# A two-layer retention and DeltaNet trunk on one core: two TensorE turns of the DeltaNet steps go by VectorE and DRAM, two sums of squares go to ScalarE

## The chip, the cores and the metric

The kernel runs on one core of a Trainium2 chip. The core has five engines that run side by side, each with its own queue of instructions: TensorE (PE in the profile, with its weight loads as PEld), VectorE (DVE), ScalarE (ACT), GpSimd (POOL) and SyncE (SP), which only issues transfers here. ScalarE's queue issues transfers too. Engines wait for each other by semaphores. The metric is the device time of one execution in microseconds; lower is better.

## What is computed

Two layers work on 1024 tokens of width 1024. Each normalises its input, multiplies it by one wide projection, and feeds a retention branch (4 heads) and a gated DeltaNet branch (8 heads of 128 channels). Both are gated, lifted, merged and projected back. The change touches the DeltaNet branch, cut here to what matters:

```python
qkv = silu(causal_conv(concat([dq, dk, dv]), conv_w))
q = l2norm(q) * DN_DK ** -0.5;  k = l2norm(k)
# chunks of tokens, per head: L from k k^T, beta and decay; (I + L) solved by blocks for u and w
v_new = u_n - w_n @ state
o     = q_dec @ state + attn @ v_new
state = state * exp(g_last) + k_dec^T @ v_new
o_d = o * rsqrt(mean(o * o) + EPS) * dn_gain      # normed per token and head
o_d = o_d * silu(dz)                              # the gate
```

## The kernel before

All the large products are three-pass ones: each operand is split in a high and a low part, and three matmuls of 128x512 stand for one (lines 866, 868 and 870). Channels lie on partitions and tokens along the row, except inside the DeltaNet steps, where a chunk of 128 tokens lies on partitions.

The DeltaNet branch runs as **units**, half a head each (512 tokens, four chunks). A layer has one unit `first`, then for 7 heads an `even` and an `odd` unit, then `even_last` and `odd_last`. Unit t does two things at once: it runs the recurrence of half head t, and it prepares half head t + 1 (Gram matrix of the keys, the blockwise solve, the query-key product). The order of all of it is written out by hand in `unit_schedule`: 24 slots for a unit, each with some steps of the two strands and two pieces ("fill") of the projection matmuls of later heads. Every engine walks the same list and does its own part of each step; between steps it waits only for the semaphores named in its part. So a step's place in the list is its place in the queue of every engine that takes part in it. TensorE writes the projections to two PSUM banks in turn, and ScalarE or VectorE ("evac", "z_silu") must empty a bank before it is written again.

The steps that the change touches:

- `ks`, `xu`, `so` (slots 0 to 11): the recurrence over four chunks. TensorE (lines 1171, 1182, 1195 to 1202) alternates with VectorE (`ks` at 2299, `so` at 2309 and 2314) and ScalarE (`xu`, 1620).
- `kt` (slot 2): TensorE turns four 128x128 blocks of the next keys into token rows (line 1109, by the helper at 849); VectorE multiplies them, out of PSUM, with the decay into `kd` (2205). The recurrence of the next unit needs `kd`, and so does `level_v` 0.
- `vs` (slot 2): a 128x4 product on VectorE (2208). `solve` (slots 3 to 7): 30 small VectorE instructions (2280, 2283), behind the load of the blocks of L from DRAM by SP.
- `qt` (slot 4): TensorE turns the queries, ScalarE squares them (1615), VectorE sums (`qe`, 2213).
- `osq`, `og`, `on` (slots 12 to 14): ScalarE squares the unit's output out of PSUM (1625), VectorE sums along the row (2319) and adds, GpSimd takes the power (2676), VectorE multiplies into `on` (2329).
- `ob` (slot 15): TensorE turns `on` back to channels on partitions (1205), VectorE multiplies it with the gate `sz` (2333). `store` (slot 18): ScalarE's queue sends it to `o_scratch` in DRAM.
- `gram`, `diag`, `keys`, `nl` (slots 15 to 17): the Gram matrix of the keys after next on TensorE (1104) and its scalings on VectorE (2163 to 2191). `on` and the product of `diag` share one buffer.

GpSimd splits weights (2579, three times a unit), scales the queries (2672, at `qt`) and masks (2659, 2661). SP loads weights (655), rows and the blocks of L.

## Time and profile before

| | |
|---|---|
| median of three runs | 2646.9 us (2643.08 to 2647.69) |
| the profiled execution: span from first to last instruction | 2644.2 us |
| median above that span | 2.7 us |
| TensorE busy | 2620.6 us, 99% |
| VectorE busy | 1761.1 us, 67% |
| ScalarE, GpSimd busy | 704.5 and 798.6 us, 27% and 30% |
| TensorE's granted clock, mean | 0.999 of full speed |

The profile lists one execution. Its span has no further time of its own around it in the page, so it stands beside the median of the runs. A busy time is the sum of an engine's instructions; matmuls overlap in the array, so their durations can't be added up. L849 is line 849 of the kernel. `arena` is the one large SBUF buffer from which most tiles are cut, `work` and `dense_ps` are PSUM.

### The profile page before, as it was taken

Reading aid. Unit: us, or ns where it says so; the run is one execution under the profiler, and the core shown is the slowest. Engines: PE = TensorE matmul, PEld = TensorE weight load, DVE = VectorE, ACT = ScalarE, POOL = GpSimd, SP = SyncE. Lnnn points to the kernel's source line nnn. Section 1 sums busy time; section 2 is a strip of 40 time slices with the busy share of each in tenths; the row PEclk is TensorE's granted clock in tenths of the full one; section 3 lists DMA queues with packets and bytes.
Section 4 is the critical chain, followed back from the end, with each engine's and each line's share of the span. In section 5 each row is a group of like instructions: output and inputs, shape, how many; then the busy total and the mean of one; then the engine's idle time right before and its main releaser. Section 6 shows DMA issues by size and latency. Waiting matters only on the chain.

```text
span 2644.2 us, 40210 instructions
## 1 busy us (share of the span) xinstructions
PE 2620.6 (99%) x14874; PEld 2238.1 (85%) x14874; DVE 1761.1 (67%) x3972; ACT 704.5 (27%) x1440; POOL 798.6 (30%) x451
## 2 busy tenths in 40 slices
PE   8999999999999999999999999999999999999998
PEld 6888888888888899888877888888888998898887
DVE  7878777877755555434577778777877555653333
ACT  5333333333311212200143333333332221231001
POOL 3123333333312212334512233332322122132453
PEclk9999999999999999999999999999999999999999
DMA  5321222122211112433533222222222111133344
GB/s 174 100 85 58 81 69 85 53 86 65 85 50 43 41 35 76 130 96 120 157 90 88 77 74 69 73 77 72 67 77 73 43 51 43 41 106 100 99 135 152
DMA packets 293416, 217.79 MB, mean 82 GB/s; under 512 B 31747, under 2 KB 246101, under 8 KB 292965
## 3 DMA queue, kind: packets, MB, share of 16 engines
q1 hardware_dynamic: 259620, 159.07, 20.9%
q10 hardware_dynamic: 33600, 56.15, 6.3%
q8 instruction: 119, 1.95, 0.3%
q14 instruction: 77, 0.62, 0.1%
HBM read 176.30 MB, written 38.86 MB: 81 GB/s over the span
## 4 chain that ended last, share of the span: by engine, by line
PE 92%; DVE 3%; DMA 2%; issue 1%; ACT 1%; SPq 0%; POOL 0%; ACTq 0%; DVEq 0%; POOLq 0%
PE dense_ps L866 23%; PE dense_ps L870 23%; PE dense_ps L868 23%; PE work L849 3%; PE dense_ps L890 2%; PE dense_ps L891 2%; PE dense_ps L892 2%; PE work L1145 1%; PE work L1182 1%; PE work L1202 1%; PE work L1121 1%; PE work L1104 1%; PE work L1171 1%; PE work L1195 1%; PE work L1156 1%
## 5 line engine op out<-in xcount | busy, mean ns | idle before, releaser
L866 PE MATMUL dense_ps<-act_hi,w_hi 128*128 128x512 f32 x2552 | 1048.3, 411 | 1.7 <-DVE w_lo L1797 0.8
L870 PE MATMUL dense_ps<-act_hi,w_lo 128*128 128x512 f32 x2552 | 998.4, 391 | 0.0
L868 PE MATMUL dense_ps<-act_lo,w_hi 128*128 128x512 f32 x2552 | 997.3, 391 | 0.0
L2579 POOL TENSOR_TENSOR w_lo<-w_raw,w_hi 128x1024 fp32r<-128x1024 f32 x162 | 400.1, 2470 | 1024.5 <-ACT w_hi L1429 582.7
L870 PEld LDWEIGHTS dense_ps<-act_hi,w_lo 128*128 128x128 f32 x2552 | 479.0, 188 | 105.8
L866 PEld LDWEIGHTS dense_ps<-act_hi,w_hi 128*128 128x128 f32 x2552 | 481.0, 188 | 86.9 <-POOL act_lo L2600 2.3
L868 PEld LDWEIGHTS dense_ps<-act_lo,w_hi 128*128 128x128 f32 x2552 | 481.5, 189 | 78.8 <-issue 0.5
L1973 DVE SCALAR_TENSOR_TENSOR arena<-arena,cols 128x512 f32<-128x512 f32 x288 | 244.3, 848 | 6.1
L1429 ACT ACTIVATE w_hi<-w_raw 128x1024 fp32r<-128x1024 f32 x94 | 99.1, 1054 | 330.5 <-PE dense_ps L870 310.5
L1419 ACT ACTIVATE arena<-dense_ps 128x512 f32<-128x512 f32 x96 | 57.2, 596 | 258.5 <-PE dense_ps L870 258.5
L849 PE MATMUL work<-mk,arena 128*128 128x128 f32 x768 | 112.1, 275 | 7.9 <-DMA arena<-in_x 7.9
L2280 DVE TENSOR_TENSOR arena<-arena 128x60 f32<-128x60 f32 (+14 forms) x480 | 99.9, 208 | 20.2 <-DMA arena<-l_scratch 7.8
L892 PE MATMUL dense_ps<-v_later_lo,act_hi 128*128 128x256 f32 x384 | 107.9, 281 | 0.0
L890 PE MATMUL dense_ps<-v_later_hi,act_hi 128*128 128x256 f32 x384 | 107.9, 281 | 0.0
L891 PE MATMUL dense_ps<-v_later_hi,act_lo 128*128 128x256 f32 x384 | 107.9, 281 | 0.0
L849 PEld LDWEIGHTS work<-mk,arena 128*128 128x128 f32 x768 | 91.8, 142 | 17.7 <-issue 5.2
L2283 DVE TENSOR_TENSOR arena<-arena 128x60 f32<-128x60 f32 (+14 forms) x480 | 92.4, 192 | 16.5
L2666 POOL TENSOR_TENSOR arena<-arena,negh 128x4 f32<-128x4 f32 x32 | 33.0, 1032 | 230.1 <-DVE arena L2180 230.1
L866 PE MATMUL dense_ps<-o_hi,w_hi 128*128 128x512 f32 x256 | 99.6, 389 | 0.0
L868 PE MATMUL dense_ps<-o_lo,w_hi 128*128 128x512 f32 x256 | 99.6, 389 | 0.0
L870 PE MATMUL dense_ps<-o_hi,w_lo 128*128 128x512 f32 x256 | 99.6, 389 | 0.0
L1620 ACT ACTIVATE arena<-work 128x128 f32<-128x128 f32 x128 | 34.9, 273 | 229.7 <-PE work L1182 224.4
(262 smaller groups left out, 4094.7 us busy)
## 6 DMA issues: line engine op xcount, KB each, us to landing
w_raw<-in_w_in SPq DMA_DIRECT2D x138, 512.0 KB, 3.8
arena<-l_scratch SPq DMA_DIRECT2D x64, 256.0 KB
arena<-gate_scratch ACTq DMA_DIRECT2D x64, 256.0 KB, 2.7
gate_scratch<-arena ACTq DMA_DIRECT2D x36, 256.0 KB, 2.0
w_raw<-in_w_out SPq DMA_DIRECT2D x18, 512.0 KB, 3.7
o_scratch<-arena ACTq DMA_DIRECT2D x32, 256.0 KB, 2.2
w_raw<-in_w_up_dn SPq DMA_DIRECT2D x16, 512.0 KB, 3.6
arena<-o_scratch ACTq DMA_DIRECT2D x32, 256.0 KB, 3.7
```

The costliest lines, as they stand in the source:

```text
L849: mm = eng.transpose(wk[bank][:, c * P:(c + 1) * P], src, ident)
L866: eng.matmul(dense_ps[:, to, :], w_hi[:, slot, k, :], hi[:, k, seg], start=(k == 0), stop=False)
L868: eng.matmul(dense_ps[:, to, :], w_hi[:, slot, k, :], lo[:, k, seg], start=False, stop=False)
L870: mm = eng.matmul(dense_ps[:, to, :], w_lo[:, slot, k, :], hi[:, k, seg], start=False, stop=(k == KT - 1))
L890: eng.matmul(dst, act_hi[:, k, tok], hi[:, k, :], start=(k == 0), stop=False)
L891: eng.matmul(dst, act_lo[:, k, tok], hi[:, k, :], start=False, stop=False)
L892: mm = eng.matmul(dst, act_hi[:, k, tok], lo[:, k, :], start=False, stop=(k == KT - 1))
L1429: eng.activation(w_hi[:, slot, :, :], w_raw[:, :, :], ACT.Copy).then_inc(w_hi_ok.sem, 1)
L1973: eng.scalar_tensor_tensor(out=acc[:, i % 2, :], in0=src, scalar=wcol, in1=acc[:, i % 2, :], op0=ALU.mult, op1=ALU.add).then_inc(conv_s.se ...
L2280: eng.tensor_tensor(xm[:, :, 0:left], column, xs[:, :, k:k + 1].to_broadcast([P, CPH, left]), ALU.mult).then_inc(sv_s.sem, 1)
L2283: eng.tensor_tensor(xs[:, :, k + 1:BASE], xs[:, :, k + 1:BASE], xm[:, :, 0:left], ALU.add)\
L2579: eng.tensor_tensor(w_lo[:, slot, :, :], w_from[second][:, :, :], w_hi[:, slot, :, :].bitcast(F32), ALU.subtract)\
```

## The change

In the units `even` and `odd`, the turn of the normed output (`ob`) leaves TensorE; the turn of the keys (`kt`) leaves it in all `odd` units and in the `even` ones from the second head on. In their place VectorE transposes the 32x32 blocks of both (`turn_o` in slot 15, `turn_k` in slot 17), ScalarE's queue stores the blocks to DRAM in four transfers that put each block at its turned place (`put`, slot 18; runs of 32 floats, 128 B) and, when these have landed, loads both tiles back as whole rows (`get`, slot 21; runs of 512 B). The next unit's `kd` product reads the keys from there, and the gate product of the output (`late_ob`) is done in slot 3 of the next unit, its store (`late_store`) in slot 10. The two squares are done by ScalarE in four pieces of 128x128 with a sum each, and VectorE's two row sums go. Three semaphores are merged into one to make room; this adds no wait.

```diff
@@ unit_schedule (kinds that end in "last" keep "ob" and "store")
-        at(18, "store")
+            at(18, "store")
+        if kind in ("even", "odd"):
+            at(3, "late_ob")
+            at(10, "late_store")
+        elif kind == "even_last":
+            at(1, "late_ob")
+            at(3, "late_store")
...
-        begin(15, 1, ("ob",))
+        begin(15, 1, ("turn_o",))
+        at(17, "turn_k")
+        at(18, "put")
+        at(21, "get")
@@ TensorE
                         elif what == "kt":
+                            if kind == "odd" or kind == "even" and h:
+                                continue
...
                             if t is not None:
-                                eng.wait_ge(ob_ok.sem, ob_ok.after(t, 0))
+                                eng.wait_ge(on_ok.sem, on_ok.after(t, 0))
@@ ScalarE
-                            eng.activation(sq, wk[1 + nb][:, :], ACT.Square).then_inc(sq_ok.sem, 1)
+                            for c in range(CPH):
+                                ins = eng.activation(sq[:, c * P:(c + 1) * P], wk[1 + nb][:, c * P:(c + 1) * P], ACT.Square,
+                                                     accum_out=qss[:, c:c + 1])
+                            ins.then_inc(sq_ok.sem, 1)
...
+                        elif what == "put":
+                            u = back(l, h, b)
+                            ms = slice(0, 2 * CPH * CPH)
+                            eng.wait_ge(on_ok.sem, on_ok.after(t, BACK + 1))
+                            eng.wait_ge(back_in.sem, back_in.after(u, 0))
+                            for i in range(CPH):
+                                rows = slice(32 * i, 32 * i + 32)
+                                eng.dma_start(back_dram[ms, :, rows].rearrange("m r s -> r m s"), turned[rows, ms, :])\
+                                   .then_inc(back_st.sem, 16)
+                        elif what == "get":
+                            u = back(l, h, b)
+                            eng.wait_ge(back_st.sem, back_st.after(u, 64))
+                            eng.wait_ge(kd_ok.sem, kd_ok.after(tn, 1))
+                            eng.wait_ge(ob_ok.sem, ob_ok.after(t, 0))
+                            eng.dma_start(tokens[:, 0:2].rearrange("p x c t -> p (x c) t"),
+                                          back_dram[0:2 * CPH * CPH, :, :].rearrange("(m j) r d -> (j r) m d", j=CPH))\
+                               .then_inc(back_in.sem, 16)
@@ VectorE ("diag" of the next keys, then "kt", "qe", "og" and the new steps)
+                            if step[1] and t is not None:
+                                eng.wait_ge(on_ok.sem, on_ok.after(t, 2))
...
-                            eng.tensor_tensor(kd[nb], chunks(4), per_token(hs[:, 3, ns_of]), ALU.mult).then_inc(kd_ok.sem, 1)
+                            if kind == "odd" or kind == "even" and h:
+                                eng.wait_ge(back_in.sem, back_in.after(back(l, h, b) - 1, 16))
+                                src = tokens[:, BACK_K]
...
+                            eng.tensor_tensor(kd[nb], src, per_token(hs[:, 3, ns_of]), ALU.mult).then_inc(kd_ok.sem, 1)
...
-                            eng.tensor_reduce(qss, sq.rearrange("p (c t) -> p c t", c=CPH), mybir.AxisListType.X, ALU.add)\
-                               .then_inc(qe_s.sem, 1)
...
-                            eng.tensor_reduce(og[:, 0, :], osq.rearrange("p (c t) -> p c t", c=CPH), mybir.AxisListType.X,
-                                              ALU.add).then_inc(og_s.sem, 1)
...
+                        elif what == "turn_o":
+                            eng.wait_ge(on_ok.sem, on_ok.after(t, 1))
+                            eng.transpose(turned_of(BACK_O), on.rearrange("p c t -> p (c t)")).then_inc(on_ok.sem, 1)
+                        elif what == "turn_k":
...
+                            eng.transpose(turned_of(BACK_K), kqv[:, 0, b * HALF:(b + 1) * HALF]).then_inc(on_ok.sem, 1)
+                        elif what == "late_ob":
...
+                            eng.wait_ge(back_in.sem, back_in.after(back(l, h, b) - 1, 16))
+                            eng.scalar_tensor_tensor(out=sz[:, seg], in0=tokens[:, BACK_O].rearrange("p c t -> p (c t)"),
+                                                     scalar=dngh[:, 0:1], in1=sz[:, seg],
+                                                     op0=ALU.mult, op1=ALU.mult).then_inc(ob_ok.sem, 1)
```

## Rows read from the trace of the kernel before

**Rows 1.** The page: busy us (share of span) xinstructions; chain of waits by engine.
```profile
PE 2620.6 (99%) x14874; PEld 2238.1 (85%) x14874; DVE 1761.1 (67%) x3972; ACT 704.5 (27%) x1440; POOL 798.6 (30%) x451
...
PE 92%; DVE 3%; DMA 2%; issue 1%; ACT 1%; SPq 0%; POOL 0%; ACTq 0%; DVEq 0%; POOLq 0%
```
**Rows 2.** Busy us by stretch: length, engines (instructions), TensorE clock, DMA share, GB/s.
```profile
594.00:660.00 66.00, 66.00 (x403) 56.56 (x402) 52.22 (x136) 21.99 (x49) 19.97 (x12) 1.00 0.22 65
```
**Rows 3.** Timeline of TensorE, 365 to 372 us: start, us, engine, line, operation.
```profile
365.42 0.39 PE L1202 MATMUL work<-arena 128*128 128x128 f32 x2
365.64 0.60 PE L849 MATMUL work<-mk,arena 128*128 128x128 f32 x4
365.99 0.47 PE L866 MATMUL dense_ps<-act_hi,w_hi 128*128 128x512 f32 x1
...
369.08 0.38 PE L1182 MATMUL work<-arena 128*128 128x128 f32 x2
...
371.55 0.39 PE L1202 MATMUL work<-arena 128*128 128x128 f32 x2
371.69 0.48 PE L866 MATMUL dense_ps<-act_hi,w_hi 128*128 128x512 f32 x1
```
**Rows 4.** Timeline of TensorE, 347 to 376 us, groups of eight records.
```profile
347.54 1.11 PE L1104 MATMUL work<-arena 128*128 128x128 f32 x8
348.48 0.60 PE L849 MATMUL work<-mk,arena 128*128 128x128 f32 x4
348.84 0.48 PE L866 MATMUL dense_ps<-act_hi,w_hi 128*128 128x512 f32 x1
...
374.99 1.06 PE L1121 MATMUL work<-arena 128*128 128x128 f32 x8
375.80 0.47 PE L866 MATMUL dense_ps<-act_hi,w_hi 128*128 128x512 f32 x1
```
**Rows 5.** Groups by line and shape, whole span: busy us, mean ns, idle before.
```profile
L849 PE MATMUL work<-mk,arena 128*128 128x128 f32 x768 | 112.1, 275 | 7.9 <-DMA arena<-in_x 7.9
...
L2237 DVE STREAM_TRANSPOSE arena<-arena 32x128 f32<-32x128 f32 x128 | 38.5, 301 | 1.8 <-DVE arena L2149 0.4
...
L1620 ACT ACTIVATE arena<-work 128x128 f32<-128x128 f32 x128 | 34.9, 273 | 229.7 <-PE work L1182 224.4 <-ACT arena L1419 5.3
...
L2333 DVE SCALAR_TENSOR_TENSOR arena<-work,dngh,arena 128x512 f32<-128x512 f32 x32 | 24.0, 750 | 22.9 <-PE work L849 22.9
...
L2319 DVE TENSOR_REDUCE arena<-arena 128x4 f32<-128x512 f32 x32 | 21.9, 683 | 2.3
```
**Rows 6.** Timeline of VectorE, 366 to 398 us.
```profile
366.28 0.69 DVE L2205 TENSOR_TENSOR arena<-work,arena 128x512 f32<-128x512 f32 x1 [0.37 <-PE work L849]
366.88 1.23 DVE L2208 SCALAR_TENSOR_TENSOR arena<-arena 128x4 f32<-128x4 f32 x1
368.03 0.34 DVE L2299 SCALAR_TENSOR_TENSOR arena<-work,arena 128x128 f32<-128x128 f32 x1
...
397.17 1.13 DVE L2189 SCALAR_TENSOR_TENSOR arena<-work,arena 128x128 f32<-128x128 f32 x4
```
**Rows 7.** Timeline of GpSimd, 364 to 368 us.
```profile
364.45 2.40 POOL L2579 TENSOR_TENSOR w_lo<-w_raw,w_hi 128x1024 fp32r<-128x1024 f32 x1 [8.65 <-ACT w_hi L1429]
366.80 1.29 POOL L2672 TENSOR_TENSOR arena<-arena 128x512 f32<-128x512 f32 x1
```
**Rows 8.** One line's instructions, whole span: duration ns min/median/max, first and last start.
```profile
L1383 ACT ACTIVATION_READ_ACCUMULATOR arena<-arena x8: 185/188/193, 6.1 to 21.6; 128x1 f32 x8
```
**Rows 9.** Timeline of ScalarE around 406 us.
```profile
405.92 0.63 ACT L1435 ACTIVATE arena<-arena 128x512 f32<-128x512 f32 x1 [2.59 <-DVE arena L1973]
```
**Rows 10.** Busy by stretch, as rows 2, with stores of L's blocks under way.
```profile
62.00:62.50 0.50, 0.50 (x4) 0.40 (x3) 0.50 (x2) 0.00 (x0) 0.00 (x0) 1.00 0.20 19
```
**Rows 11.** DMA: a queue (packets, MB, share of 16 engines); issues, KB, us to landing.
```profile
q1 hardware_dynamic: 259620, 159.07, 20.9%
...
w_raw<-in_w_in SPq DMA_DIRECT2D x138, 512.0 KB, 3.8
```

More of the change, by code:

```diff
@@ L47 @@
 HBUF = 4
+BACK = 2
+BACK_O, BACK_K = range(BACK)
+BACK_UNITS = 2 * (DH - 1)
 def in_order(*steps):
@@ L81, with __init__, Later @@
 class Signal:
-    def __init__(self, handle, per):
-        self.sem, self.per = handle, per
+    def __init__(self, handle, per, before=0):
+        self.sem, self.per, self.count = handle, per, before
     def after(self, t, k):
-        return t * self.per + (self.per + k)
+        return t * self.per + (self.per + self.count + k)
+def Later(first, before):
+    return Signal(first.sem, first.per, first.count + before)
 def constants():
@@ L629, in is_v, with back @@
             return BLK_RET + 2 <= idx < BLK_UPD and (idx - BLK_RET) % 6 in (2, 3)
+        def back(l, h, b):
+            return l * BACK_UNITS + 2 * h + b
         def evacuated(i, a):
@@ L2022, in ret_rope @@
                     seg = slice(b * HALF, (b + 1) * HALF)
+                    if t % RH == 0 and i == 0:
+                        eng.wait_ge(ob_ok.sem, ob_ok.after(l * (2 * DH) + BACK_UNITS - 1, 1))
                     eng.wait_ge(swap_ok.sem, swap_ok.after(t, 2 * i + 2))
@@ L2201, in delta_unit @@
                                 eng.wait_ge(zeros_ok.sem, zeros_ok.after(l, 2))
-                            eng.wait_ge(kt_ps.sem, kt_ps.after(tn, 1))
+                            if kind == "odd" or kind == "even" and h:
+                                eng.wait_ge(back_in.sem, back_in.after(back(l, h, b) - 1, 16))
+                                src = tokens[:, BACK_K]
+                            else:
+                                eng.wait_ge(kt_ps.sem, kt_ps.after(3 * l + ("first", "even", "even_last").index(kind), 1))
+                                src = chunks(4)
                             if t is not None:
                                 eng.wait_ge(st_ps.sem, st_ps.after(t, 0))
-                            eng.tensor_tensor(kd[nb], chunks(4), per_token(hs[:, 3, ns_of]), ALU.mult).then_inc(kd_ok.sem, 1)
+                            eng.tensor_tensor(kd[nb], src, per_token(hs[:, 3, ns_of]), ALU.mult).then_inc(kd_ok.sem, 1)
                         elif what == "vs":
```

56 lines of the change are left out of this document (39 added, 17 removed).

## The prediction, made before the run

> **What bounds the kernel now.** I began with the page's busy line and its chain of waits: TensorE is busy 99% of the span and 92% of the chain that ended last is TensorE's own work [rows 1]. I then took a table of busy time by stretch, because the change touches only the DeltaNet steps: in a 66 us stretch in the middle of them, TensorE is busy for all 66.00 us, VectorE for 52.22, ScalarE for 21.99 and GpSimd for 19.97 [rows 2]. So in these steps TensorE's stream sets the time, every other engine has idle time, and what is taken out of that stream is gained unless another engine becomes late by it.
>
> How much TensorE time a turn costs isn't read from its busy time. The group of all turns shows 768 instructions of 275 ns [rows 5]; by that the 216 turns that go would be worth 59 us. But records of pipelined matmuls overlap, so the busy time counts the same moment more than once. The timeline tells it, by when the next instruction starts.
>
> **What goes from TensorE.** Two turns of four 128x128 blocks.
> Keys ("kt"): the last matmul of a recurrence step starts at 365.42, the turn at 365.64, the next projection matmul at 365.99, which is 0.57 us from the first to the third. Where no turn lies between, the same pair starts at 371.55 and 371.69, 0.14 us apart [rows 3]. A turn of keys costs 0.43 us. It goes in all 7 odd units of a layer and in 6 of its 7 even ones: 13 times 2 layers is 26, and 26 x 0.43 = 11.2 us.
> Output ("ob"): it stands behind the next keys' Gram matmuls. Gram starts at 347.54, the turn at 348.48, the next projection matmul at 348.84: 1.30 us. A group of the same eight records without a turn behind it takes from 374.99 to 375.80, 0.81 us [rows 4]. A turn of the output costs 0.49 us. It goes in 14 units of a layer: 28 x 0.49 = 13.7 us.
> Together 24.9 us, the most the change can give by removed work; TensorE's waits on VectorE are next to nothing in these steps [rows 2], so there is no wait to win back.
>
> **What is added to VectorE.** Per unit two transposes of 128x512 in blocks of 32x32 come in, and two sums along rows go, 683 ns each for this shape [rows 5]. No 128x512 transpose is in the trace. The 32x128 one takes 301 ns [rows 5]. The lower bound is what every other one-pass instruction on 128x512 takes, 0.68; the upper is four times the small one, 1.20. I take 0.70, since an instruction with a quarter of the columns and less than half the time points to a fixed part. So VectorE's sum is level (2 x 0.70 against 2 x 0.68; at the upper bound 1.0 us more), and with 13.8 us idle in 66 it does not become the bound as a sum. What matters is where the work lies.
>
> The transposes and the missing sums lie in the last third of a unit, where the output's norm is waited for by nothing on TensorE once the turn is gone; the next Gram product's diagonal then waits on VectorE's own transpose, queued right in front of it. I cost them at nothing; their cover is VectorE's idle time.
>
> The gate product moves from the end of a unit to slot 3 of the next, right in front of the 15 solve steps, on the engine that at that point alternates with TensorE. It takes 0.75 us [rows 5]. And the decayed keys ("kt" on VectorE) now read their keys from SBUF instead of PSUM. Two rows show what this may do: GpSimd runs from 364.45 to 366.85 and from 366.80 to 368.09 [rows 7], and the VectorE instruction just behind the decayed keys, a 128x4 one that reads only SBUF, starts at 366.88 and lasts 1.23 us, up to 368.11, the end of GpSimd's second one; the decayed keys in front of it, reading PSUM, were not held and took 0.69 [rows 6]. So a VectorE instruction that reads two operands from SBUF waits out a GpSimd one. The Trainium skill says this as a rule and it speaks against the change (SBUF — State Buffer, "Who interferes with whom"): a VectorE instruction with two SBUF inputs contends with a GpSimd one that reads SBUF, and one with a single SBUF input doesn't. By that rule both moved products can now be held, which neither could before, and the sum loses what follows; without it the sum would be the full 24.9. The row agrees.
>
> What it costs here: whether they start at 366.28 as now or earlier, the turn being gone, the decayed keys are held until 366.85 and end at about 367.4 instead of 366.97; GpSimd's next instruction and the 128x4 one behind it shift by about 0.35, and so does the first product of the recurrence (368.03, ended 368.37 [rows 6]). TensorE needs that product at 369.08 [rows 3], now at 368.65, the turn being gone. 368.72 against 368.65 is a stall of 0.1 us; behind it the gate product's 0.75 is taken up by the gaps between the solve steps, or partly not. In the other kind of unit the same comparison starts with less slack. I take 0.3 us for each of 28 units, 8 us; the bounds are 0 and the whole 0.9 us that a unit gains.
>
> **What is added to ScalarE.** Each of the 64 squares becomes four of 128x128 with a sum: 273 ns for one of that shape [rows 5] and 188 ns for reading the accumulator [rows 8], 4 x 0.46 = 1.84 us at most in place of one pass. ScalarE is idle two thirds of the time [rows 2], and the next to wait for either square has another engine's work in between; nothing on the path. Its cover is that idle time; without it up to 1.8 us twice a unit would show.
>
> **The trip through memory.** ScalarE's queue also gets four stores ("put", slot 18), a load ("get", slot 21) and the later store of the output. The put waits for VectorE's second transpose, the get for the landing of the put, so everything behind the get on ScalarE waits too: the copies that free TensorE's PSUM banks, then the splitting of weights and the recurrence's copies. In an even unit VectorE ends its Gram products at 397.17 + 1.13 = 398.30 [rows 6] and the second transpose at 399.0. ScalarE's first instruction behind the get starts at 405.92 now [rows 9]. So the trip has 6.9 us.
> The put is 4096 packets of 128 B, 256 on each of the 16 DMA engines. The kernel before moves nothing in packets of that size. In a stretch with 64-byte packets alone the engines are busy 0.20 at 19 GB/s [rows 10]: 0.20 x 16 x 64 B / 19 GB/s = 10.8 ns. On SP's queue, mostly of 512 B and longer, the mean is 20.9% of 16 x 2644.2 us over 259620 packets = 34 ns [rows 11]. These are the bounds, 2.8 and 8.7 us. The fixed part: a weight load of 1024 packets lands in 3.8 us [rows 11], 64 x 34 ns = 2.2 are transfer, 1.6 remain. By bytes (613 B the queue's mean) 128 B lie at 13.5 ns, 3.5 us, so the put lands at 399.0 + 1.6 + 3.5 = 404.1, 1.8 us early; if it shares the engines with a whole weight load, at 406.3, 0.4 late. I cost the trip at nothing in the forecast, being nearer to the 64-byte row by size. The get, like a weight load, takes 3.8 us: from 405.9 it lands at 409.7, before the next unit's decayed keys want it.
> The Trainium skill warns of such packets (DMA: Bandwidth & Descriptors, "Specifications"): under 512 B the DMA engines read, modify and write. No run here shows it for 128 B; a doubled price would be rival two.
>
> **The sum.** -24.9 + 8 = -17 us. The profile's span is 2644.2, the median of the runs 2646.9, 2.7 above it; the sum is carried over as it is: 2630.
>
> **The rivals.**
> One: nothing is held up, the whole 24.9 come: 2622. For it: VectorE has 13.8 us idle in 66 [rows 2], and the gate product goes from a place where it waited for the turn. Against it: the held row.
> Two, slower: the put lands late and the get blocks ScalarE. It decides from (6.9 - 1.6) / 256 = 21 ns for a packet, or earlier if a weight load shares the engines. At 24 ns, halfway between 13.5 and 34, the put lands at 406.7 alone and 408.9 beside a load, 1.9 us late on average; with about 1 us less in the odd units 1.4 on average, and 28 x 1.4 = 39 us lost for 17 gained: 2669. At 34 ns it would be over 2690. For it: the slack is small against the unknown. Against it: the 64-byte row, and engines that are mostly idle.
> Three: the held keys and the moved gate product push every unit by the 0.9 us that it gains: 2647, no change. For it: between slots 2 and 9 VectorE and TensorE answer each other with slacks of a few tenths.
> That the change doesn't do what it says: the turns are replaced but TensorE waits for the same data, which is rival three with another name.
>
> **How the numbers follow.** Forecast 0.42 (2630), one 0.22 (2622), three 0.14 (2647), two 0.22 (2669 and around). Faster by over 0.2% (5.3 us, about what a measurement of this kernel can tell from no change) is the forecast and one, 0.64; same is three, 0.14; slower is two, 0.22. The range runs from 2619 (a little under the full gain) to 2662, which takes in three and the milder half of two and leaves out some 0.12 above and 0.04 below. The forecast's own range is 2622 to 2640.
>
> **What would show it.** Right: 216 turns fewer in TensorE's group; its stream still without gaps; the decayed keys and the gate product longer than 0.69 and 0.75 us in some units; the put landing some 5 us after its first issue; no ScalarE wait for a DMA of over half a microsecond. Wrong: TensorE waiting for a ScalarE copy at the start of units (two), TensorE waiting for VectorE's recurrence products (three), or transposes near 1.2 us.

## The result and the profile after

Measured: 2651.2 us against 2643.3 for the kernel before, ratio 1.0024 with a 95% interval of 1.0015 to 1.0033. Forecast were 2630 us and a gain; the time lies inside the range, the sign is wrong: the change loses some 6 us, with an interval of 4 to 9. The profile of the kernel before has one wait of 4.4 us, at 1412 us in the first even unit of the second layer, where the other profiles have at most 0.5; so the times of the runs are compared, and not the profiles' spans.

The page of the changed kernel: busy us (share of the span) and instructions, the chain of waits by engine and by line; under it groups by line (busy us, mean ns, idle before).

```profile
span 2646.6 us, 40476 instructions
PE 2609.5 (99%) x14658; PEld 2211.7 (84%) x14658; DVE 1773.1 (67%) x3962; ACT 740.7 (28%) x1888; POOL 814.0 (31%) x451
...
PE 79%; DVE 7%; DMA 6%; issue 2%; SPq 2%; POOL 1%; ACT 1%; ACTq 1%; DVEq 0%; POOLq 0%
...
L875 PE MATMUL work<-mk,arena 128*128 128x128 f32 x552 | 80.4, 278 | 7.1 <-DMA arena<-in_x 7.1
L2274 DVE TENSOR_TENSOR arena<-arena 128x512 f32<-128x512 f32 x26 | 38.1, 1466 | 1.0 <-DMA arena<-back_scratch 1.0
L2403 DVE STREAM_TRANSPOSE arena<-arena 128x512 f32<-128x512 f32 x26 | 18.1, 694 | 0.0
L2409 DVE SCALAR_TENSOR_TENSOR arena<-arena,dngh 128x512 f32<-128x512 f32 x28 | 22.1, 790 | 0.8 <-DMA arena<-back_scratch 0.8
```

The 216 turns are gone (768 in [rows 5], 552 here), and the transposes cost what they should. But where the chain was TensorE's to 92% [rows 1], it is now to 79%, and VectorE and DMA have what is missing. The decayed keys, L2274, take 1.47 us in place of 0.69 [rows 6]. TensorE waits (waited for: us in total, times, longest) at two places of the recurrence where it hardly waited before:

```profile
PE work L1210 <- DVE arena L2365: 9.3, 18, 1.1
PE work L1199 <- DVE arena L2380: 7.1, 10, 1.2
```

VectorE's part of an even unit, and what the other queues do beside it (start, us, engine, line; the same place as [rows 3, 6, 7]):

```profile
354.28 2.28 ACTq L1665 DMA_DIRECT2D back_scratch<-arena  x4
355.18 0.38 SPq L681 DMA_DIRECT2D w_raw<-in_w_in  x1
355.65 4.54 SPq L751 DMA_DIRECT2D l_scratch<-arena  x8
361.41 0.39 ACTq L1672 DMA_DIRECT2D arena<-back_scratch  x1
362.48 1.21 SPq L759 DMA_DIRECT2D arena<-l_scratch  x2
364.25 2.39 POOL L2661 TENSOR_TENSOR w_lo<-w_raw,w_hi 128x1024 fp32r<-128x1024 f32 x1 [9.10 <-ACT w_hi L1457]
365.65 1.55 DVE L2274 TENSOR_TENSOR arena<-arena 128x512 f32<-128x512 f32 x1
366.60 1.76 POOL L2754 TENSOR_TENSOR arena<-arena 128x512 f32<-128x512 f32 x1
367.12 1.25 DVE L2277 SCALAR_TENSOR_TENSOR arena<-arena 128x4 f32<-128x4 f32 x1
368.30 0.34 DVE L2365 SCALAR_TENSOR_TENSOR arena<-work,arena 128x128 f32<-128x128 f32 x1
368.56 0.74 DVE L2409 SCALAR_TENSOR_TENSOR arena<-arena,dngh 128x512 f32<-128x512 f32 x1
370.21 0.26 DVE L2346 TENSOR_TENSOR arena<-arena 128x60 f32<-128x60 f32 x1 [0.92 <-DMA arena<-l_scratch]
```

Two things are to be seen. First, the decayed keys start 0.63 us sooner than before and run beside GpSimd's product up to 367.20; the small product behind them then runs into GpSimd's next one, so that the recurrence's product L2365 starts at 368.30 instead of 368.03 [rows 6], though TensorE now comes for it 0.43 us sooner. Second, the solve, from L2346 on, stands still for 0.92 us: what ends the wait is not VectorE but the load of L's blocks from memory. Behind the solve's first steps in VectorE's queue stands L2380, the product that TensorE (L1199) waits for ahead of slot 6.

For all runs I compared TensorE's stream with that of the kernel before: the mean time between the starts of successive groups of projection matmuls (two groups to a slot), over 26 units (12 even and 14 odd ones; the first even unit of each layer, which keeps its turn of the keys, is left out), as a difference in us by place. An even unit works on the first half of a head, an odd one on the second. Both turns taken out show as -0.44 each in every run that has no such turn; the rest are new stalls (places under 0.05 left out; "ahead of 6" sums slots 6 and 7):

```
                     even units                         odd units
                     ahead of slot        net           ahead of slot          net
after                4: .35  6: .77       +.28          1: .18  4: .75         +.10
squares                                    .00                                 +.03
out_only                                  -.43                                 -.42
keys_only            4: .35  6: .07        .00          4: .63                 +.18
no_put               4: .35  6: .14       -.34          1: .06  4: .60         -.17
late_kd              6: 1.34              +.50          1: .18  4: .12  6: .12 -.40
one_input            4: .40  6: .60       +.19          1: .62  4: .13         -.09
early                4: .38  6: 3.33     +2.90          1: .98  4: .81         +.94
late_kd_early        6: 3.79             +2.94          1: .99  4: .22  6: .05 +.45
keys_late                                 -.41          4: .06                 -.36
late_get             6: .31  9: .21  10: .17  -.14      1: .12  9: .23  10: .54  +.09
split                9: .21  10: .17      -.46          9: .21  10: .39        -.26
split7                                    -.83                                 -.81
```

In the changed kernel the nets, 12 x 0.28 + 14 x 0.10 = 4.8 us for the 26 units, are most of the 6 us that the runs show. The work did leave TensorE; the stalls ahead of slots 4 and 6 took it back.

### The profile page after: what moved, and what is told of

Read it like the earlier page. It is cut to its first block, busy times and chain, and to the rows that moved or that the text cites. A ratio compares the mean times of both kernels' runs of the same rounds, so it can differ in the third digit from the quotient of the medians.

```text
span 2646.6 us, 40476 instructions
## 1 busy us (share of the span) xinstructions
PE 2609.5 (99%) x14658; PEld 2211.7 (84%) x14658; DVE 1773.1 (67%) x3962; ACT 740.7 (28%) x1888; POOL 814.0 (31%) x451
## 4 chain that ended last, share of the span: by engine, by line
PE 79%; DVE 7%; DMA 6%; issue 2%; SPq 2%; POOL 1%; ACT 1%; ACTq 1%; DVEq 0%; POOLq 0%
PE dense_ps L892 19%; PE dense_ps L896 19%; PE dense_ps L894 19%; DMA arena<-l_scratch 3%; PE dense_ps L916 2%; PE dense_ps L917 2%; PE dense_ps L918 2%; PE work L875 2%; SPq L751 1%; DMA l_scratch<-arena 1%; PE work L1210 1%; PE work L1173 1%; PE work L1149 1%; DVE arena L2274 1%; PE work L1184 1%
## 5 line engine op out<-in xcount | busy, mean ns | idle before, releaser
L1447 ACT ACTIVATE arena<-dense_ps 128x512 f32<-128x512 f32 x96 | 57.1, 595 | 251.5 <-PE dense_ps L896 238.1
L2346 DVE TENSOR_TENSOR arena<-arena 128x60 f32<-128x60 f32 (+14 forms) x480 | 100.3, 209 | 26.3 <-DMA arena<-l_scratch 13.9
L1847 DVE CAST w_hi<-w_raw 128x1024 fp32r<-128x1024 f32 x82 | 56.5, 688 | 59.2 <-PE dense_ps L896 43.3
L1569 ACT ACTIVATE arena<-dense_ps 128x512 f32<-128x512 f32 x64 | 38.3, 599 | 193.5 <-PE dense_ps L896 193.5
```

Source lines behind the costliest of these rows:

```text
L1447: eng.activation(raw[:, j % 2, 3 + b * HALF:3 + (b + 1) * HALF], dense_ps[:, b, :], ACT.Copy)\
L2346: eng.tensor_tensor(xm[:, :, 0:left], column, xs[:, :, k:k + 1].to_broadcast([P, CPH, left]), ALU.mult).then_inc(sv_s.sem, 1)
```

## The experiments

**Which part loses.** Three kernels with one part each.

squares: the kernel before, with the sums made by ScalarE (the norm of the output likewise).

```diff
-                            eng.activation(sq, wk[1 + nb][:, :], ACT.Square).then_inc(sq_ok.sem, 1)
+                            for c in range(CPH):
+                                ins = eng.activation(sq[:, c * P:(c + 1) * P], wk[1 + nb][:, c * P:(c + 1) * P], ACT.Square,
+                                                     accum_out=qss[:, c:c + 1])
+                            ins.then_inc(sq_ok.sem, 1)
...
-                            eng.tensor_reduce(qss, sq.rearrange("p (c t) -> p c t", c=CPH), mybir.AxisListType.X, ALU.add)\
-                               .then_inc(qe_s.sem, 1)
```

> The kernel before, with one part of the change alone: the sums of squares made by ScalarE's four accumulating activations, VectorE's two reductions (2 x 0.68 us a unit) gone. Theory (the loss comes from the trip: late blocks of L, held keys, the moved gate product): the squares cost nothing, since VectorE loses as much as ScalarE gains and TensorE waited under 5 us for VectorE before; 2639 to 2645 us, ratio 0.998 to 1.001. Rival S (ScalarE's longer squares, some 1.1 us in place of one 0.7 us activation, stand in its queue ahead of work that TensorE waits for, 0.3 us a unit): about 2652 us, ratio 1.003, TensorE's waits for ScalarE longer by about 8 us.

Ratio 0.9997, 0.9988 to 1.0006. The squares neither cost nor bring anything; rival S falls.

out_only: the changed kernel, keys turned by TensorE.

```diff
-                            if kind == "odd" or kind == "even" and h:
-                                continue
                             eng.wait_ge(vv_ok.sem, vv_ok.after(tn, 0))
                             turn(4, [ch(0, c) for c in range(CPH)]).then_inc(kt_ps.sem, 1)
...
-        at(17, "turn_k")
...
-                            ms = slice(0, 2 * CPH * CPH)
+                            ms = slice(0, CPH * CPH)
```

> The changed kernel with the keys turned by TensorE again, so that the trip through memory carries the output alone: the turn of the keys is back (0.44 us x 26 on TensorE), VectorE's second transpose is gone, the decayed keys read PSUM again, half the put's packets. Theory: the held keys go back from about 1.5 to 0.69 us, the blocks of L come earlier by about half of their 0.9 us, the moved gate product (0.75 us ahead of the solve, against 0.68 us of reductions saved) stays; TensorE wins 28 x 0.44 = 12 us and gives about half of it back: 2635 to 2643 us, ratio 0.997 to 1.000. Rival G (the moved gate product alone sets the delay of the solve): no better than the changed kernel plus 11 us less its key term, 2648 to 2656 us.

2629.9 us, ratio 0.9944, 0.9932 to 0.9957: 14.8 us gained (11 to 18 by the interval), more than theory allowed and all that the turn is worth (28 x 0.44 = 12.3). The gate product stands ahead of the solve here too and costs nothing: rival G falls, and so does my own supposition that half of the gain would go on it. The decayed keys, reading PSUM, are back at their old time, and the product behind them too:

```profile
L2267 DVE TENSOR_TENSOR arena<-work,arena 128x512 f32<-128x512 f32 x32 | 22.2, 692 | 13.5 <-PE work L874 13.4
L2270 DVE SCALAR_TENSOR_TENSOR arena<-arena 128x4 f32<-128x4 f32 x32 | 26.7, 834 | 0.0
```

keys_only: the changed kernel, output turned by TensorE, multiplied and stored in the old place.

```diff
-        begin(15, 1, ("turn_o",))
+        begin(15, 1, ("ob",))
...
-                            ms = slice(0, 2 * CPH * CPH)
+                            ms = slice(CPH * CPH, 2 * CPH * CPH)
```

> The changed kernel with the output turned back by TensorE and multiplied by its gate and stored in its old place, so that the trip carries the keys alone: TensorE wins 26 x 0.43 = 11 us, half the put's packets, no gate product ahead of the solve, but the decayed keys still have two SBUF inputs. Theory: the decayed keys still take about 1.5 us beside GpSimd's two-input product in place of 0.69; VectorE has 1.36 us of reductions less, so that the solve starts about 0.2 us later than in the kernel before or level with it; 2636 to 2646 us, ratio 0.997 to 1.001. Rival K (the held keys are the whole loss, 0.8 us a unit): 2648 to 2656 us. Rival G (the gate product is the loss): 2632 us.

2647.6 us, ratio 1.0011, 1.0002 to 1.0020, just above theory's range and just below rival K's. The keys' part loses its 11 us and about 3 more. The decayed keys and the product behind them, against 0.69 and 0.86 us in the kernel before:

```profile
L2265 DVE TENSOR_TENSOR arena<-arena 128x512 f32<-128x512 f32 x26 | 37.8, 1452 | 0.0
L2268 DVE SCALAR_TENSOR_TENSOR arena<-arena 128x4 f32<-128x4 f32 x32 | 34.0, 1063 | 0.0
```

The stalls ahead of slot 4 are 0.35 and 0.63 us, those of the whole change but for a little. Ahead of slot 6 there is next to none. So the two parts, -14.8 and +2.9, don't add up to +6.3: together they cost 18 us that neither costs alone.

**What the two parts share: the trip's traffic.** no_put writes the turned blocks in the first unit only.

```diff
-                            for i in range(CPH):
+                            for i in range(CPH if u == 0 else 0):
...
+                            if u:
+                                eng.sem_inc(back_st.sem, 64)
```

> The changed kernel with the turned blocks written to memory in the first unit alone (later units read those again: the output and the keys of later units are stale). All else stands: the transposes, the load of the rows, the held keys, the moved gate product. Theory: the put's 4096 packets a unit stand in the same 16 DMA engines as the blocks of L that the solve waits for; without them the solve's 0.9 us wait for the blocks goes in the even units (14 x 0.9 = 13 us), and the half of it that the held keys and the gate product would have cost anyway shows: 2634 to 2642 us, VectorE's wait for the blocks of L back from 13.9 to about 8 us. Rival K+G (the held keys and the gate product set the solve's start in both kinds of unit, the DMA traffic nothing): 2648 to 2653 us.

2637.3 us, ratio 0.9974, 0.9963 to 0.9985: 13 us less than the changed kernel, as theory said; rival K+G falls. The stall ahead of slot 6 goes from 0.77 to 0.14 us, which is 12 x 0.63 = 7.6 us, and those ahead of slot 4 stay or nearly so, which parts the two causes. The odd units' stalls ahead of slots 1 and 4 fall by 14 x (0.12 + 0.15) = 3.8 us. VectorE's wait for the blocks of L, in the changed kernel and here:

```profile
DVE arena L2346 <- DMA arena<-l_scratch: 13.9, 14, 1.8
```
```profile
DVE arena L2348 <- DMA arena<-l_scratch: 7.8, 8, 1.7
```

In the 12 even units alone these waits fall from 8.9 to 1.2 us; the rest are in first and last units.

How full the DMA engines are shows where the blocks lose time. The 18 us from 355 us on in the kernel before, then the same place in the changed one, in 40 slices (DMA: busy tenths of the 16 engines):

```profile
DMA  0000489991000000247999454554269999931100
...
DMA packets 3425, 2.41 MB, mean 134 GB/s; under 512 B 736, under 2 KB 2784, under 8 KB 3424
```
```profile
DMA  0299879999999510008479999956358999976411
...
DMA packets 8618, 3.43 MB, mean 191 GB/s; under 512 B 4911, under 2 KB 7983, under 8 KB 8618
```

The weight load that took the engines for 2 us before now shares them with the put for 5, and the stores of L's blocks, next in SyncE's queue, come out behind both. SyncE waits for them before it issues the load of the blocks. The Trainium skill (DMA: Bandwidth & Descriptors, "Queues, rings and completion order") adds that a DMA's semaphore lands only after every earlier write of the same DMA engine, on whichever queue; no run here parts that from the sharing of the engines. From the issue of the weight load to that of L's blocks it is 362.48 - 355.18 = 7.3 us in the changed kernel. In the kernel before it is 5.3 us, and in out_only, with half of the bytes, 6.0:

```profile
355.82 0.38 SPq L655 DMA_DIRECT2D w_raw<-in_w_in  x1
...
361.14 1.21 SPq L733 DMA_DIRECT2D arena<-l_scratch  x2
```

```profile
352.94 0.38 SPq L680 DMA_DIRECT2D w_raw<-in_w_in  x1
...
358.96 1.21 SPq L758 DMA_DIRECT2D arena<-l_scratch  x2
```

But late stores alone are not what costs. In no_put, too, it is 7.25 us from the weight load to the load of L's blocks, since the get, with no put to wait for, goes out in the put's place:

```profile
353.96 0.38 SPq L681 DMA_DIRECT2D w_raw<-in_w_in  x1
356.82 0.40 ACTq L1674 DMA_DIRECT2D arena<-back_scratch  x1
361.21 1.21 SPq L759 DMA_DIRECT2D arena<-l_scratch  x2
```

What goes there is the second delay: in the changed kernel the get is issued 1.1 us ahead of the load of L's blocks (361.41 and 362.48), and this load then takes longer. The semaphore events of the traces tell when the load landed; means over the 12 even units, in us (late_kd and late_get are described below; - is under 0.05):

```
                                             before  after  late_kd  no_put  late_get  out_only  split7
weight load to issue of L's load               5.4    7.2     7.1      7.4      7.3       6.2      6.2
L's load, issue of second half to landing      5.6    6.8     7.0      5.8      5.9       5.8      5.4
landing, after the unit's first xu             3.9    6.4     6.6      5.5      5.6       4.3      4.1
TensorE's stall ahead of slot 6                       .77    1.34      .14      .31       -        -
```

So in the changed kernel the blocks land 2.5 us later in the unit than before: 1.8 by their stores, which come behind the put, and 1.2 by the get ahead of their load, less the 0.4 by which the weight load goes out sooner. With the first alone they land 1.6 us later, and nearly no stall is left: the unit has that much room. So the late stores alone don't make the stall; the get's delay on top of them does. No run has the get's delay alone.

**Why the decayed keys are long.** Two kernels: late_kd has the same instruction at a time when GpSimd is idle; one_input has it in the old place, with GpSimd's first product there made a copy.

```diff
+        at(7, "late_kd")
         at(7, "kq")
...
                             if kind == "odd" or kind == "even" and h:
-                                eng.wait_ge(back_in.sem, back_in.after(back(l, h, b) - 1, 16))
-                                src = tokens[:, BACK_K]
...
+                                continue
...
+                        elif what == "late_kd":
...
+                            eng.wait_ge(back_in.sem, back_in.after(back(l, h, b) - 1, 16))
+                            eng.wait_ge(st_ps.sem, st_ps.after(t, 0))
+                            eng.tensor_tensor(kd[nb], tokens[:, BACK_K], per_token(hs[:, 3, ns_of]), ALU.mult).then_inc(kd_ok.sem, 1)
```

> The changed kernel with one step moved: the decayed keys of the units that take them from the trip are made at the head of slot 7, where VectorE waits 0.8 to 1.0 us for TensorE and GpSimd is idle, in place of slot 2 beside GpSimd's product. Same instruction, same two SBUF inputs. Theory H (two SBUF inputs are held while GpSimd runs a product of two SBUF inputs): the instruction takes about 0.74 us there, as the gate product does, in place of 1.47; the small products behind it in slot 2 start some 0.7 us sooner than in the kernel before, and TensorE's stalls ahead of slot 4 (0.35 us in even units, 0.63 in odd ones by the run with the keys alone) go: 14 x 0.98 = 14 us; the wait for the blocks of L in the even units stays: 2634 to 2642 us. Rival D (two SBUF inputs are slow wherever they stand): 1.5 us in slot 7 too, 0.7 of it in the way of the solve: 2642 to 2650 us. Rival P (the put's traffic alone holds the loop, whatever VectorE does): 2648 to 2654 us.

```diff
-                eng.tensor_tensor(w_lo[:, slot, :, :], w_from[second][:, :, :], w_hi[:, slot, :, :].bitcast(F32), ALU.subtract)\
-                   .then_inc(w_lo_ok.sem, 1)
+                eng.tensor_copy(w_lo[:, slot, :, :], w_from[second][:, :, :]).then_inc(w_lo_ok.sem, 1)
```

> The changed kernel with GpSimd's low half of a weight block (w_raw less w_hi, two SBUF inputs, 2.4 us) written as a copy of w_raw (one input, same size): the low halves are wrong numbers, the work of the other engines is the same. The decayed keys stay in slot 2. Theory H: a GpSimd instruction with one input doesn't hold VectorE's two-input product, so that the decayed keys take 0.7 to 0.9 us on the mean in place of 1.47, as far as they don't meet GpSimd's other two-input product. Rival D (the form is slow in itself): 1.4 to 1.5 us. If GpSimd's copy still holds the port: 1.2 us or more.

The decayed keys in late_kd, then in one_input, with GpSimd's copy:

```profile
L2279 DVE TENSOR_TENSOR arena<-arena 128x512 f32<-128x512 f32 x26 | 17.8, 684 | 0.0
```
```profile
L2274 DVE TENSOR_TENSOR arena<-arena 128x512 f32<-128x512 f32 x26 | 21.1, 812 | 30.5 <-DMA arena<-back_scratch 30.4
L2661 POOL CAST w_lo<-w_raw 128x1024 fp32r<-128x1024 f32 x162 | 183.1, 1130 | 1175.2 <-ACT w_hi L1457 668.8 <-DVE w_hi L1847 506.3
```

late_kd has 684 ns in place of 1466, and none of its 26 decayed keys meets a GpSimd instruction: the form is not slow, it is held by GpSimd's two-input product. Rival D falls, and the hold of theory H is shown. The rule of the Trainium skill (SBUF — State Buffer, "Who interferes with whom") agrees.

one_input (one run, 2644.5 us, no verdict) shows less than it was made for. The copy takes 1.13 us instead of 2.48 and is over before the decayed keys start, in all 26 units; the keys also wait 30.4 us in all for the get. So no run has the decayed keys beside a GpSimd instruction of one input, and what that does is not shown. But in some units the keys meet GpSimd's next product, of two inputs: the 7 that start 0.18 to 1.02 us ahead of its end take 0.73 to 1.57 us, each of them the time to that end and 0.55 us; the other 19, clear of it or at most 0.11 us from its end, take 0.69.

The time of late_kd is another matter: 2642.8 us, ratio 0.9992, 0.9983 to 1.0001, just outside theory's range and inside that of rival D, whose reason the 684 ns have ruled out. The stall ahead of slot 4 went in the even units and mostly in the odd ones, but in the even units the stall ahead of slot 6 grew from 0.77 to 1.34 us. VectorE came to the solve sooner and waited longer for the blocks:

```profile
DVE arena L2351 <- DMA arena<-l_scratch: 27.2, 17, 2.7
```

So in the changed kernel's even units the late blocks covered the held keys' harm. Curing one shows the other.

**Can the trip go at another time?** early begins it sooner, late_kd_early does both.

```diff
-        begin(15, 1, ("turn_o",))
-        at(17, "turn_k")
-        at(18, "put")
-        at(21, "get")
+        begin(15, 1, ("turn_o", "turn_k"))
+        at(16, "put")
+        at(20, "get")
```

> The changed kernel with the trip begun sooner: the keys' transpose right behind the output's in slot 15, the put in slot 16, the get in slot 20. Theory (the put's packets stand ahead of the stores of L, which are issued 1.4 us behind the first put): with the put over some 3 us sooner the stores of L land in 2.1 to 2.5 us again, the solve's wait for the blocks falls from 13.9 to 5 to 8 us in all, and TensorE's stall ahead of slot 6 in the even units (0.77 us x 14 = 11 us) goes, as without the put: 2636 to 2642 us. Rival (the amount of packets counts and not when they go, since they now meet the loads of the weights): no change, 2648 to 2654 us.

> Both moves together: the decayed keys in slot 7 and the trip begun sooner. Theory (the held keys and the put's collision with the blocks of L are the whole of what ate the gain): TensorE keeps its 24.9 us of removed turns but for a few: 2619 to 2626 us. Rival (a third cost, such as the gate product ahead of the solve, is left under both): 2630 to 2640 us.

2698.4 us, ratio 1.0198 (1.0185 to 1.0212), and 2701.0, ratio 1.0210 (1.0196 to 1.0224). Both misses, theory and rival. The step in slot 17 that splits a weight block now stands behind the put on ScalarE (early, an odd unit):

```profile
359.00 2.46 ACTq L1664 DMA_DIRECT2D back_scratch<-arena  x4
361.58 1.06 ACT L1456 ACTIVATE w_hi<-w_raw 128x1024 fp32r<-128x1024 f32 x1 [3.11 <-issue]
362.72 2.70 POOL L2660 TENSOR_TENSOR w_lo<-w_raw,w_hi 128x1024 fp32r<-128x1024 f32 x1 [1.85 <-ACT w_hi L1456]
365.45 0.38 SPq L680 DMA_DIRECT2D w_raw<-in_w_in  x1
365.92 3.80 SPq L750 DMA_DIRECT2D l_scratch<-arena  x8
```

Four issues take 2.46 us of ScalarE's queue; the split, GpSimd's part of it, SyncE's next weight load and the stores of L's blocks behind that follow one another. VectorE's wait for the blocks is 41.1 us here. In the changed kernel the put stands behind this split. That this order is the cause is read from the trace; no run moved the split alone.

late_get leaves the put, and moves the get behind the load of L's blocks (decayed keys in slot 8, gate product in slot 13).

```diff
         if kind in ("even", "odd"):
-            at(3, "late_ob")
-            at(10, "late_store")
+            at(4, "get")
+            at(13, "late_ob")
+            at(14, "late_store")
         elif kind == "even_last":
-            at(1, "late_ob")
-            at(3, "late_store")
+            at(1, "get")
+            at(4, "late_ob")
+            at(6, "late_store")
...
-        at(21, "get")
```

> The whole change with the decayed keys in slot 8 and the load of the rows (the get) moved from slot 21 to slot 4 of the next unit, behind the load of L's blocks; the gate product goes to slot 13, the store behind it to 14 (in the last even unit of a layer to slots 1, 4 and 6). The put stays in slot 18. Theory G (the get's 512 KB stand ahead of the load of L's blocks, which SyncE issues 1.1 us behind it): the solve's wait for the blocks, 27.2 us with the decayed keys in slot 7, falls below 10 us and TensorE keeps most of its 24.9 us: 2620 to 2628 us. Theory P (the put's packets make the stores of L's blocks land 1.3 us later, and so the load is issued later): the wait for the blocks stays above 15 us: 2634 to 2643 us. Both in parts: 2628 to 2634 us.

2649.7 us, ratio 1.0018, 1.0010 to 1.0027, outside of all three. Against late_kd, the wait for the blocks fell only from 27.2 to 23.2 us, and their load is issued as late as before: theory P. But the load now lands 1.0 us sooner (the table above), and TensorE's stall ahead of slot 6 fell from 1.34 to 0.31 us: theory G. Both count, and the get's move cures most of that stall. What spoilt the time is elsewhere. The stalls ahead of slots 9 and 10 take 12 x 0.38 + 14 x 0.77 = 15 us, 2.5 of them in a single odd unit that has more than the others; split has 12 x 0.38 + 14 x 0.60 = 13 there, and lost them when its decayed keys left slot 8. The last even units of the two layers, where the edit puts get, gate product and store in other slots, are 3.3 and 2.7 us longer than in the kernel before; why, no run tells.

**Half of the bytes, and the keys out of GpSimd's way.** keys_late is keys_only with the decayed keys in slot 7, the edit of late_kd.

> The run with the keys alone, with the decayed keys moved from slot 2 to slot 7 (0.68 us there, by the run that moved them under the whole change, in place of 1.47). Theory: the run with the keys alone lost TensorE's 11 us to the held keys and to nothing else, so that nearly all of it comes back with them in slot 7, and half of the trip's bytes hold nothing: 2632 to 2638 us, ratio 0.995 to 0.998. Rival (half of the trip's bytes make the blocks of L late too, and the stall shows ahead of slot 6 as soon as slot 3 is free): 2640 to 2647 us.

2634.4 us, ratio 0.9962, 0.9950 to 0.9973: 10 us gained, against 3 lost with the same kernel's keys in slot 2. So the keys' part loses by the held product, 13 us of it, and by nothing else of weight.

split has the whole change, the trip in two halves. The output's is as in out_only; SyncE issues the keys' put behind its load of L's blocks and the get behind its row load; decayed keys in slot 8. split7 is split with them in slot 7.

```diff
+                def key_put(u):
...
+                    for i in range(CPH):
+                        rows = slice(32 * i, 32 * i + 32)
+                        eng.dma_start(back_dram[ms, :, rows].rearrange("m r s -> r m s"), turned[rows, ms, :])\
+                           .then_inc(back_st.sem, 16)
...
                     l_blocks(2 * h + 2, 0)
+                    key_put(2 * h)
                     load_w(m + BLK_HEADS + 5, w_src(l, w_in, GR0 + P + h * P))
                     row_load(h + 1, 1)
+                    key_get(2 * h)
```

> The whole change with the trip in two halves at two times: the output's as in the run with the output alone (put in slot 18, get in slot 21, gate product in slot 3), the keys' put and get issued by SyncE behind its load of L's blocks and its next row load, and the decayed keys in slot 8 (0.7 us). Theory (the amount of the trip's packets that fall between the weight load and the load of L's blocks decides; half of them cost nothing): TensorE keeps its 24.9 us less 0 to 6: 2619 to 2626 us. Rival (the keys' 2048 packets meet the load of L's blocks itself, or the four issues on SyncE's queue hold the next weight load): 2630 to 2645 us.

> The run with the trip in two halves, with the decayed keys moved from the head of slot 8 to the head of slot 7, where VectorE stands idle for 0.97 us (374.09 to 375.06 us in the profile of that run) and the load of the keys' rows, issued at 368.66 us and landing 4.8 us later, is just in. Theory (the stalls of the run with two halves, 0.2 us ahead of slot 9 and 0.15 to 0.38 us ahead of slot 10, are the 0.69 us of the decayed keys ahead of the levels' chain and nothing else): these go, 14 x (0.59 + 0.33) = 13 us, TensorE keeps its 24.9 us: 2619 to 2625 us, faster than the run with the output alone (2629.9). Rival (the keys' rows land after the idle time, so that VectorE waits in slot 7 for them): 2630 to 2640 us.

split: 2635.2 us, ratio 0.9960, 0.9947 to 0.9973. split7: 2623.8 us, ratio 0.9922, 0.9908 to 0.9935. In split the stall ahead of slot 6 is gone, as the theory of the bytes has it, but its time is the rival's: the stalls ahead of slots 9 and 10 were there, for neither of the rival's reasons. Moving the decayed keys by one slot took them away. split7 beats the kernel before by 21 us and out_only by 6; its page and its wait for the blocks:

```profile
PE 2600.2 (99%) x14658; PEld 2215.4 (85%) x14658; DVE 1759.5 (67%) x3962; ACT 739.4 (28%) x1888; POOL 800.8 (31%) x451
...
PE 93%; DVE 2%; DMA 2%; ACT 1%; issue 1%; SPq 0%; ACTq 0%; DVEq 0%; POOL 0%
...
DVE arena L2381 <- DMA arena<-l_scratch: 2.6, 2, 1.3
```

The chain is TensorE's to 93% again. It moves the same bytes through memory as the changed kernel. What the change was short of was room for them, not a cheaper trip.

## Why the prediction was wrong

**TensorE's removed work: right.** 0.43 and 0.49 us a turn were forecast, each measured 0.44. By that the sum is 54 x 0.44 = 23.8 us in place of 24.9.

**VectorE's transposes and ScalarE's squares: right.** 0.694 us where 0.70 was taken; the squares cost nothing (squares). Their pieces start about 0.25 us apart, so that four end within 1.15 us, not 1.84.

**The gate product: right, by out_only.** It stands in slot 3 there and costs nothing. In rival three it was named as half of the cause; it isn't.

**The held keys: the mechanism right, the size too small.** I took 0.3 us a unit, 8 us. The stalls ahead of slot 4 in keys_only are 12 x 0.35 + 14 x 0.63 = 13.0 us, and keys_late gives 13 back. I ended the decayed keys at 367.4 and so let the products behind them shift by 0.35; they do end at 367.20, a little sooner, but GpSimd's second product, 1.29 us in [rows 7], became 1.76 beside VectorE's and so held the 128x4 product up to 368.37. And I worked out the even unit only; of the odd one I wrote that it had less slack and gave it no number, and it has the larger stall.

**The trip through memory: the step that failed.** I gave it a deadline at one place, the get on ScalarE, and costed it at nothing since that deadline held. The price of a packet was right, 13 ns at the median where 13.5 was taken; a doubled price did not show. The put, issued from 399.04 us on in the even unit, let the get go at 405.94, 6.9 us later and on the deadline: later than the 5.1 us forecast for it alone, sooner than the 7.3 beside a whole weight load. ScalarE's first instruction behind it starts 0.5 us late (406.43 in place of 405.92 [rows 9]). No wait of TensorE for ScalarE of over 0.2 us follows directly, but VectorE waits for that instruction, and so its next product of the recurrence is 0.5 us late; first the changed kernel, then the kernel before:

```profile
405.94 0.39 ACTq L1672 DMA_DIRECT2D arena<-back_scratch  x1
406.43 0.63 ACT L1463 ACTIVATE arena<-arena 128x512 f32<-128x512 f32 x1 [2.85 <-DVE arena L2029]
407.09 0.69 DVE L2043 SCALAR_TENSOR_TENSOR arena<-arena 128x512 f32<-128x512 f32 x1 [0.96 <-ACT arena L1463]
```
```profile
406.59 0.69 DVE L1987 SCALAR_TENSOR_TENSOR arena<-arena 128x512 f32<-128x512 f32 x1 [0.70 <-ACT arena L1435]
```

This is the stall ahead of slot 1 in the odd units, 14 x 0.18 = 2.5 us; without the put VectorE's wait is back at 0.70. So rival two's way was there, a small part of the loss and by way of VectorE. What I didn't follow is what else stands in the 16 DMA engines at that time: SyncE's weight load, behind it in the same queue the stores of L's blocks, whose landing SyncE waits for, and behind the get the load of these blocks, for which the solve waits. "Engines that are mostly idle" was read from a mean; in this stretch they are the limit. The stall that this makes, ahead of slot 6 in the even units, is 12 x 0.77 = 9 us, and the run without the put is 13 us faster in all. Rival two had the trip as the culprit, but made ScalarE the one to wait and a packet's price the point of decision; the larger part came by the blocks of L, at the price forecast.

**The sum with the measured terms.** -23.8 for the turns, +13.0 for the held keys, +13 for the put and what hangs on it, and some 2.5 for what no_put still loses ahead of slots 1 and 6 (12 x 0.14 + 14 x 0.06): +4.7, inside the measured 6.3 with its interval of 4.0 to 8.7. The forecast of 2630 stood on a median of 2646.9 for the kernel before; on the 2643.3 measured beside the change the same -17 gives 2626, so the changes are compared here, -17 and +6. Of these 23 us between forecast and result 5 are a term that was mis-sized, and most of the rest is a wait of which no term was made. Rival three, no change by pushes of 0.9 us a unit, came nearest in effect, at a chance of 0.14, and for half of the reason.

**What stays open.** By landings the put's share of the late blocks is 1.8 us and the get's 1.2, but the stall is not their sum, since the unit has room for the first; no run has the second alone, and late_get moved the decayed keys and the gate product as well. The 0.15 us that no_put takes off the stall ahead of slot 4 in the odd units was not traced to one cause. Whether the stores are late by shared engines or by the order of completion was not parted either.

## What to carry to other kernels

When work goes from a compute engine to a trip through memory, list the transfers that are on the DMA engines and in each issuing queue at that time, and follow those that someone waits for, not only the trip's own landing; a mean DMA share says nothing of the one stretch. When an operand moves from PSUM to SBUF, look at what GpSimd does at that moment, and place the instruction where GpSimd is idle. Both cures are a matter of place: the same instructions and the same bytes went from 6 us lost to 21 us gained.

## What the runs showed of the hardware

- A VectorE product of two SBUF inputs that starts while GpSimd runs one of its own is held: in the changed kernel, begun 0.99 us ahead of the end of GpSimd's (364.25 to 366.64), it took 1.55 us, in one_input begun 1.02 and 0.59 us ahead 1.57 and 1.14; with GpSimd idle 0.68. GpSimd's next one, begun in the midst of VectorE's, took 1.76 instead of 1.29. With one input from PSUM it wasn't held: 0.69, begun 0.57 us ahead of GpSimd's end [rows 6, 7].
- 512 KB more between a weight load and the stores behind it in its queue delay what waits for these by 1.8 to 2.0 us (medians of even and odd units), whether in 4096 packets of 128 B (the changed kernel's put) or in 1024 of 512 B (no_put's get); 256 KB by 0.8 to 1.1. The half costs this kernel nothing.
- A load of 512 KB from ScalarE's queue, issued 1.1 us ahead of the load of L's blocks, makes this one take about 1.1 us longer (6.8 to 7.0 us in place of 5.8 to 5.9).
- Four stores of 1024 packets take 2.3 us of the issuing queue (2.46 in early), a load of the same bytes in longer packets 0.39. early, in which they stand ahead of a weight split, is 47 us slower than the changed kernel.
